# Part of the sparse tokens' first-level choice moved into the query projection, with the end of the picks and a load order changed

## The reference

```python
def peer_ffn(h, w_query, sub_keys, expert_u, expert_v):   # shortened
    q = (xt @ w_query).reshape(T, 8, 2, 128)               # 8 heads, 2 halves: 16 rows a token
    scores = einsum('thpc,hpnc->thpn', q, sub_keys)         # 128 keys for each of the 16 rows
    top_s, top_i = top_k(scores, 16)                        # FIRST level: 16 of 128, 16 times a token
    cand_s = top_s[:, :, 0, :, None] + top_s[:, :, 1, None, :]
    best_s, best_pos = top_k(cand_s..., 16)                 # SECOND level: 16 pairs a head
    idx  = ...                                              # 8 x 16 = 128 experts a token, of 16384
    gate = softmax(best_s)
    y = sum over the 128: gate * gelu(x . expert_u[idx]) * expert_v[idx]
```

## Time and profile before

| | us |
|---|---|
| median of 3 runs (2687.11 to 2694.08) | 2687.2 |
| the profiled execution, its own time | 2686.54 |
| its span, from which all rows are | 2684.8 |
| PE busy | 2316.3 (86%) |
| DVE busy | 1514.0 (56%) |
| ACT busy | 631.7 (24%) |
| POOL busy | 601.3 (22%) |

### The profile page before, as it was taken

The page is one execution under the profiler, slowest core; times in us unless marked ns, Lnnn a source line. Parts: engine busy times, 40 slices in busy tenths (PEclk is TensorE's granted clock), DMA queues, the critical chain, the costliest instruction groups (busy, mean ns, idle before and its releaser), DMA issues. The chain is left out here.

```text
span 2684.8 us, 42381 instructions
## 1 busy us (share of the span) xinstructions
PE 2316.3 (86%) x16668; PEld 1693.7 (63%) x16668; DVE 1514.0 (56%) x2992; ACT 631.7 (24%) x1540; POOL 601.3 (22%) x637
## 2 busy tenths in 40 slices
PE   8989988999998689997998788768998799788873
PEld 8988865555554387886964445428788796455431
DVE  5787643110000155588966666675558896666666
ACT  4543322000000035222311111114622231111111
POOL 0011200111111100001234545530000123545553
PEclk9999989999999989999999999999999899999998
DMA  7420026999999781379999999978137899999996
GB/s 230 144 68 3 3 110 249 401 419 419 418 420 419 316 288 32 118 255 364 361 398 408 407 405 411 389 279 287 32 118 281 341 377 397 407 411 405 410 387 254
DMA packets 223238, 794.92 MB, mean 296 GB/s; under 512 B 37909, under 2 KB 103957, under 8 KB 165312
## 3 DMA queue, kind: packets, MB, share of 16 engines
q1 hardware_dynamic: 148496, 443.86, 43.0%
q0 software_dynamic: 74544, 348.34, 32.9%
HBM read 881.07 MB, written 11.27 MB: 332 GB/s over the span
## 5 line engine op out<-in xcount | busy, mean ns | idle before, releaser
L2472 PE MATMUL psum<-v_raw,act 128*128 128x512 f32 x1024 | 504.9, 624 | 168.7 <-DMA v_raw<-expert_v_dram,all_gates 168.4
L2439 PEld LDWEIGHTS psum<-all_gates 128*128 128x128 f32 x4096 | 491.6, 195 | 103.8 <-issue 58.4
L2439 PE MATMUL psum<-all_gates 128*128 128x128 f32 x4096 | 499.8, 279 | 39.6 <-DMA all_gates<-expert_u_dram 39.1
L2582 POOL DMA_INDIRECT all_gates<-expert_pairs_dram,all_gates x256 | 261.8, 1023 | 1143.0 <-DVE all_gates L2718 533.5
L2472 PEld LDWEIGHTS psum<-v_raw,act 128*128 128x128 f32 x1024 | 181.5, 194 | 407.9 <-DMA v_raw<-expert_v_dram,all_gates 261.5
L2618 DVE CUSTOM_DVE_ANT_0 all_gates<-all_gates,psum 128x1024 f32<-128x1024 f32 x204 | 249.1, 1221 | 307.5 <-DMA all_gates<-expert_pairs_dram,all_gates 307.4
L2629 DVE SCALAR_TENSOR_TENSOR psum<-all_gates,psum 128x1024 f32<-128x1024 f32 x254 | 326.3, 1285 | 8.1 <-ACT all_gates L2543 7.8
L1741 PE MATMUL psum<-piece_raw,tile_cols 128*64 128x256 f32 x2496 | 289.3, 383 | 17.9 <-DMA piece_raw<-w_up_dram 7.8
L1741 PEld LDWEIGHTS psum<-piece_raw,tile_cols 128*64 128x64 f32 x2496 | 177.2, 137 | 130.3 <-issue 36.7
L2590 POOL DMA_INDIRECT v_raw<-expert_v_dram,all_gates x236 | 234.5, 994 | 77.7 <-issue 69.0
L2541 ACT ACTIVATE all_gates<-all_gates 128x1 f32<-128x1 f32 x256 | 51.8, 202 | 770.8 <-DVE all_gates L2618 770.5
(11 more groups left out here) (530 smaller groups left out, 3405.0 us busy)
## 6 DMA issues: line engine op xcount, KB each, us to landing
all_gates<-expert_u_dram SPq DMA_DIRECT2D x256, 512.0 KB, 7.7
piece_raw<-w_gate_dram SPq DMA_DIRECT2D x78, 1024.0 KB, 19.5
piece_raw<-w_up_dram SPq DMA_DIRECT2D x78, 1024.0 KB, 21.6
piece_raw<-w_down_dram SPq DMA_DIRECT2D x78, 1024.0 KB, 22.8
in_raw<-w_in_dram SPq DMA_DIRECT2D x48, 1024.0 KB, 5.2
query_raw<-w_query_dram SPq DMA_DIRECT2D x16, 1024.0 KB, 5.6
v_raw<-expert_v_dram SPq DMA_DIRECT2D x20, 512.0 KB, 8.1
w_o<-w_o_dram SPq DMA_DIRECT2D x16, 512.0 KB, 10.2
```

The lines of the kernel that those rows point to most:

```text
L2439: last = nc.tensor.matmul(PS[:, bank, 0:P], raw_u[:, n % RAW_U, c * P:(c + 1) * P], h_full[:, c, :], start=(c == 0), stop=(c == KD - 1), s ...
L2472: last = nc.tensor.matmul(PS[:, 4 + m, :], slot(n), raw_v[:, n % RAW_V, m * BANK:(m + 1) * BANK], start=(n == 0), stop=(n == N - 1), skip_ ...
L2582: nc.gpsimd.indirect_dma_start(out=ring[:, r, :, :].rearrange("p h d -> p (h d)"), out_offset=None, in_=S["pair_rows"], in_offset=bass.Ind ...
```

## The change

- `query` gets six banks for its units, and the other two for scores. Behind units 1, 3, 4, 5 and 6, PE computes the sparse tile's scores of one head each (heads 0 to 4), ACT copies them out, and DVE makes that head's first-level choice behind its work for the next slab. So 10 of the 16 rows of the sparse tile's first level are done when `small_experts` begins, and `select(0)` handles 6. PE waits for the keys before the first of these. An extra phase with three semaphores is put around `query`.
- `select(1)` takes 15 picks in between instead of 10, two of them in the middle of long groups. The loop has 97 picks left instead of 102, and they end with its step 121 instead of 126.
- `EARLY` is 68 instead of 72, `LISTS_AFTER` 41 instead of 46, and the shares and the exponentials on ACT stand behind earlier dense blocks.
- `want()`, which finds the v rows that are needed, is called one step later in the loop.
- `in2` issues its ten `loads` after all 12 slabs, not between them.

```diff
 def project(..., busy=(0, 0, 0, 0), loads_last=False, heads=None):
-                    if s >= RING:
+                    if s >= RING and not loads_last:
                         for buffer, src in loads[(s - RING) * share:(s - RING + 1) * share]:
                             sp.dma_start(buffer, src).then_inc(loaded, 16)
+                for buffer, src in loads if loads_last else ():
+                    sp.dma_start(buffer, src).then_inc(loaded, 16)
...
+                    if heads and n in heads.behind:        # ACT, last in unit n
+                        heads.scalar(act, heads.behind.index(n))
...
+                    if heads and n in heads.behind:        # DVE, behind low_of_slab
+                        heads.vector(dve, heads.behind.index(n))
...
+                    if heads and n in heads.behind:        # PE, behind unit n
+                        if n == heads.behind[0]:
+                            pe.wait_ge(loaded, 16 * len(loads))
+                        if act_upto[n]:
+                            pe.wait_ge(unit_act, act_upto[n])
+                        pe.wait_ge(unit_dve, n - act_upto[n])
+                        heads.tensor(pe, heads.behind.index(n))
...
+HEADS_BEHIND = (1, 3, 4, 5, 6)
+class FirstChoice:
+    def tensor(self, pe, h):      # two 128x128 products into bank 6 + h % 2
+    def scalar(self, act, h):     # waits for them, copies 256 columns to S["sc"]
+    def vector(self, dve, h):     # waits for the copy
+        for i in two: last = nc.vector.max(val[:, i, 0:8], sc[:, 1, i, :])
+        step(last)
+        for i in two: last = nc.vector.max_index(...)
+        step(last)
+        for i in two: last = nc.vector.match_replace(...)
+        step(last)
+        for i in two: last = nc.vector.max(val[:, i, 8:16], ...)
+        step(last)
+        for i in two: last = nc.vector.max_index(...)
...
-EARLY = 72
+EARLY = 68
...
-    EXP_AFTER = (14, 41)
-    LISTS_AFTER = 46
+    CHOSEN_FIRST = (2 * len(HEADS_BEHIND), 0)
+    BATCHES = tuple(range(c // 4, 4) for c in CHOSEN_FIRST)
+    EXP_AFTER = (8, 38)
+    LISTS_AFTER = 41
-    SHARES_AFTER = (24, 26, 30, 33, 34, 36, 39, 41, 43, 44)
+    SHARES_AFTER = (19, 20, 21, 23, 24, 26, 28, 29, 30, 32, 34, 35, 36, 38, 39)
-    LAST_BLOCKS = 2
+    LAST_BLOCKS = 7
...
-                    waiting = [None, None, *range(BESIDE_CHOICE)] if a == DENSE else []
+                    waiting = list(range(BESIDE_CHOICE)) if a == DENSE else []
+                    open_rows = range(CHOSEN_FIRST[turn], HP)
...
-                    if n == 0:
+                    if n == 1:
                         want()
...
-                        loads=loads, banks=(0, 1), ring=3, act_from=8,
+                        loads=loads, loads_last=True, banks=(0, 1), ring=3, act_from=8,
...
-                    above=3 * 16 * KB)
+                        above=3 * 16 * KB, banks=(0, 1, 2, 3, 4, 5),
+                        heads=FirstChoice(nc, S, head_scored, head_copied, head_chosen))
```

More of the change, by code:

```diff
@@ L196, in project @@
             raw=None, banks=tuple(range(BANKS)), ring=2, act_from=None, beside=None, norm=None,
-            ahead=None, above=0, tops_early=False, extra=None, late_loads=(), also=None, busy=(0, 0, 0, 0)):
+            ahead=None, above=0, tops_early=False, extra=None, late_loads=(), also=None, busy=(0, 0, 0, 0), loads_last=False, heads=None):
     PS, C = S["psum"], S["const"]
@@ L2271, in layer_norm, with __init__, bank, step @@
             nc.vector.tensor_scalar(norm["diag"][:, a, :], norm["ident"], norm["rstd"][:, a:a + 1], None, ALU.mult)
+HEADS_BEHIND = (1, 3, 4, 5, 6)
+class FirstChoice:
+    def __init__(self, nc, S, scored, copied, chosen):
+        self.nc, self.S, self.behind = nc, S, HEADS_BEHIND
+        self.scored, self.copied, self.chosen, self.steps = scored, copied, chosen, 0
+    def bank(self, h):
+        return self.S["psum"][:, 6 + h % 2, 0:2 * P]
+    def tensor(self, pe, h):
+        S = self.S
+        if h >= 2:
+            pe.wait_ge(self.copied, h - 1)
+        for e in range(2):
+            last = self.nc.tensor.matmul(self.bank(h)[:, e * P:(e + 1) * P], S["q_cols"][:, 2 * h + e, P:2 * P],
+                                         S["keys"][:, 2 * h + e, :], start=True, stop=True)
+        last.then_inc(self.scored, 1)
+    def scalar(self, act, h):
+        act.wait_ge(self.scored, h + 1)
+        self.nc.scalar.activation(self.S["sc"][:, 1, 2 * h:2 * h + 2, :], self.bank(h).rearrange("p (i n) -> p i n", n=P),
+                                  ACT.Copy).then_inc(self.copied, 1)
+    def vector(self, dve, h):
+        nc, sc, val, idx = self.nc, self.S["sc"], self.S["val"], self.S["idx"]
+        two = range(2 * h, 2 * h + 2)
+        def step(ins):
+            self.steps += 1
+            ins.then_inc(self.chosen, 1)
+            dve.wait_ge(self.chosen, self.steps)
+        dve.wait_ge(self.copied, h + 1)
+        for i in two:
+            last = nc.vector.max(val[:, i, 0:8], sc[:, 1, i, :])
+        step(last)
+        for i in two:
+            last = nc.vector.max_index(idx[:, i, 0:8], val[:, i, 0:8], sc[:, 1, i, :])
+        step(last)
+        for i in two:
+            last = nc.vector.match_replace(sc[:, 1, i, :], val[:, i, 0:8], sc[:, 1, i, :], NEG)
+        step(last)
+        for i in two:
+            last = nc.vector.max(val[:, i, 8:16], sc[:, 1, i, :])
+        step(last)
+        for i in two:
+            last = nc.vector.max_index(idx[:, i, 8:16], val[:, i, 8:16], sc[:, 1, i, :])
 def one_row(S, name, layer):
     return S["dram"][name][bass.ds(layer, 1), :].rearrange("l n -> (l n)").partition_broadcast(P)
-EARLY = 72
+EARLY = 68
 RAW_U, RAW_V = 4, 7
@@ L2338, in small_experts @@
         keys = S["keys"]
-        sc = spare([P, NT, HP, NKEYS])
-        val = spare([P, HP, TOPK])
-        idx = spare([P, HP, TOPK]).bitcast(U32)
+        sc, val, idx = S["sc"], S["val"], S["idx"]
         idx_h = spare([P, PH * TOPK]).bitcast(BF16).rearrange("p (h e k) -> p h e k", h=2, k=TOPK)
@@ L2417, in scores @@
                 def scores(turn, n):
-                    if turn:
-                        pe.wait_ge(scores_out, n + 1)
+                    if turn and n in BATCHES[0]:
+                        pe.wait_ge(scores_out, BATCHES[0].index(n) + 1)
                     a = ORDER[turn]
-                    for i in range(4 * n, 4 * n + 4):
+                    for i in range(max(4 * n, CHOSEN_FIRST[turn]), 4 * n + 4):
                         last = nc.tensor.matmul(PS[:, n, (i % 4) * P:(i % 4 + 1) * P], S["q_cols"][:, i, a * P:(a + 1) * P],
@@ L2477, in back @@
                         last.then_inc(y_done, 1)
-                for n in range(4):
+                for n in BATCHES[0]:
                     scores(0, n)
@@ L2482, in _ @@
                     turn_x(b)
-                for n in range(4):
+                for n in BATCHES[1]:
                     scores(1, n)
@@ L2654, in select @@
                     beside()
-                    for i in range(HP):
+                    for i in open_rows:
                         last = nc.vector.max(val[:, i, 8:16], sc[:, a, i, :])
+                        if i == middle:
+                            beside()
                     step(last)
                     beside()
-                    for i in range(HP):
+                    for i in open_rows:
                         last = nc.vector.max_index(idx[:, i, 8:16], val[:, i, 8:16], sc[:, a, i, :])
+                        if i == middle:
+                            beside()
+                    beside()
                     v = val.rearrange("p (e h) k -> p e h k", h=2)
@@ L2708, in select @@
                         step(last)
-                    beside()
+                        if width != 4:
+                            beside()
                     for h, to in enumerate((rows[:, 0, :], second)):
@@ L3040, in second_layer @@
             between["shift_row"] = spare([P, D])
-            project(nc, S, "query", S["x"], one("w_query_2", "k n"),
-                    [(c, 512, "columns") for c in range(0, 2048, 512)], evacuate=evacuate_q,
-                    raw=ahead["raw"], loads=[(S["keys"], one("sub_keys_2", "p e n"))], norm=between, ahead=ahead,
-                    above=3 * 16 * KB)
+            S["sc"] = spare([P, NT, 2 * PH, NKEYS])
+            S["val"] = spare([P, 2 * PH, TOPK])
+            S["idx"] = spare([P, 2 * PH, TOPK]).bitcast(U32)
+            with phase(nc, "head_scored head_copied head_chosen") as (_, head_scored, head_copied, head_chosen):
+                project(nc, S, "query", S["x"], one("w_query_2", "k n"),
+                        [(c, 512, "columns") for c in range(0, 2048, 512)], evacuate=evacuate_q,
+                        raw=ahead["raw"], loads=[(S["keys"], one("sub_keys_2", "p e n"))], norm=between, ahead=ahead,
+                        above=3 * 16 * KB, banks=(0, 1, 2, 3, 4, 5),
+                        heads=FirstChoice(nc, S, head_scored, head_copied, head_chosen))
```

24 lines of the change are left out of this document (14 added, 10 removed).

## The result

The changed kernel took 2654.91 us (median of four, 2652.71 to 2660.21) against 2689.51 for the kernel before, measured beside it (2687.11 to 2694.08): a ratio of 0.9887, 95% interval 0.9866 to 0.9909, so 30 us or 1.1% faster (25 to 36 us). Forecast were 2661 us, 26 less, with a range of 2648 to 2680. Run again with the last experiments it took 2656.98, ratio 0.9888 (0.9869 to 0.9907). The profiled execution took 2652.92 us with a span of 2651.1.

What follows compares the result with a forecast made beforehand. DMA was taken to bound the expert stage, PE in2 and query. Terms over two layers: in2 -12.9, query +7.4, sparse -11.0, dense -4.4, end -5.0, sum -25.9 from 2686.5, plus 0.7: 2661 us, range 2648 to 2680.

Steps and rivals of the forecast that it cites:

- in2: Projection in2: loads issued last remove PE's gaps and the clock loss behind them, 12.9 us less over both layers.
- query: Query projection: five heads' scores and choices plus an extra phase lengthen it 3.7 us a layer, 7.4 in all.
- the choices: Expert stage's sparse and dense choices: less DMA loss, 11.0 us less in the sparse and 4.4 in the dense.
- the end: End of the expert loop: picks end earlier, PE finishes 5 us behind DMA instead of 8.4; 2.5 us less a layer.
- the slabs are then never late: In in2: without loads between, a slab needs 2.7 us of DMA against a 5.76 us PE unit; all three gaps go.
- the stall of 1.0 before unit 4: In query: DVE's added choice and row work finish a slab late, so PE stalls 1.0 us.
- (e): Rival in query: the choices delay every slab by 2 us, 20 us over both layers, giving 2681; chance 0.06.
- rival (d): Dense choice: picks wait for their shares, DVE's waits for ACT 3 us or more; slower, 2703; chance 0.07.
- the 2.2 us: Dense choice: more picks in flight cut DMA's loss from 8.9 (6.0) to 6.5 (4.0) us, 2.2 a layer.
- (a): Rival: only in2 gives; the expert stage starts 3.7 us later and earlier picks' gain is eaten; 2674; chance 0.20.
- (b): Rival: the dense choice's DMA loss all but vanishes and the end gives 4 us; 2650; chance 0.12.
- (c): Rival: in2 gives nothing because PE waits for the next slab's rest instead of the copy-out; 2674; chance 0.07.

Runs made afterwards that it cites:

- no heads: Changed kernel without the five heads' choice in query, all 16 rows chosen in the expert stage, fifteen picks at later places: 2660.76 us, ratio 0.9909.
- (undone): Changed kernel with LAST_BLOCKS back at 2, so picks run to the second last block: 2666.72 us, ratio 0.9940.
- (alone): Kernel before with LAST_BLOCKS at 7 in place of 2 and nothing else: 2675.02 us, ratio 0.9970.

## Why the prediction was right, and where it was off

**The sum.** In the stages, by means over profiles: in2 -10.9, query +6.2, the choices -14.1, the end -11.1; -29.9 us in all, and the ratio gives -30. Predicted were -12.9, +7.4, -15.4 and -5.0, -25.9. Three terms were each a little too large, and one less than half its size, so the sum came out nearer than its parts.

**in2 (-12.9, measured -10.9).** The mechanism is shown: the gaps behind ACT's copy went from 4.7 and 5.2 to 0.4 and 2.3 us, and the edit alone gives its part. Off was "the slabs are then never late": `w_o` was one of two loads between the slabs. The constants, 641 KB, and some rows stand between the third slab and the fourth, which is asked for at 1805.02 and landed 13 us later. With them moved too, the stage loses 13.2 us over both layers, near what the term said. The late `w_o` cost nothing, as said: in layer 1 it was issued until 1850.2 and took at most 14.1 us, so it was there at 1864.3 at the latest. The stage's last product was at 1886.7, and the prediction's test was that `w_o` lands before it.

**query (+7.4, measured +6.2).** Units stayed at 5.76 us on PE, with no gap ahead of any; the stall of 1.0 before unit 4 didn't come. A head's choice took 2.9 us from its first maximum at 1113.13, under the 3.2 charged and short enough for DVE's copy-out to be in time. The extra phase cost 0.4 (no heads against before), not 0.8. Nothing was seen of (e): its sign, gaps before each unit, didn't appear.

**Sparse and dense choice (-15.4, measured -14.1).** The size came out, but what held the dense choice was not what the prediction said, so part of the agreement is luck. Predicted was a dense choice bound by DMA, with DVE done at 109 and DMA at 115 us behind the stage's start, and waits of DVE for ACT under 1 us. The lists came at 117.6 and 115.4, but held by DVE: PE had all its 41 blocks done and waited 7.0 and 6.1 us for DVE there. DVE was late by its 77 us of work, as sized (65 + 12), by one wait for the first share of 6.05 us (5.0 in layer 1), and by one of 2.5 (1.2) for a pick's rows. By the prediction's own sign, 3 us or more, that is rival (d)'s mechanism, once a layer and not fifteen times.

The wait goes with the first four pick loads: after them the u blocks took 11.9 us from issue to landing in the median in place of 4.6, so the gelu that the share stands behind was late. In the kernel before they slowed as much, from 4.6 to 10.9 us, behind its own first picks, but there the picks came 12 us later against the blocks, with the first share behind `gelu(24)` and not `gelu(19)`, and the first adds waited 0.1 and 1.2 us. That the u blocks slow agrees with the Trainium skill ("DMA: Bandwidth & Descriptors", Queues, rings and completion order), by which each DMA engine takes turns between the queues that have work. The prediction set that rule against the rate and against the 2.2 us. The rate rose all the same, to 391 and 381 GB/s, over the 365 of its test; whether the five picks gave any time isn't resolved. What the slower blocks touched was the order of the shares, which the prediction had among its rivals and not in its sum.

With the shares spread the stages give 4.5 us a layer more; that edit takes the wait out, has three more blocks done and frees ACT, and no run tells these three apart. Of the 7.0 us a layer that the choices gave, the heads hold 3.6 (predicted 5.5) and the five more picks 1.2, unresolved (predicted 2.2); the 2.2 us that are left are not assigned: no run takes both out at once. All three rest on one profile of a run against the mean of others.

**The end (-5.0, measured -11.1).** This is the term that was mis-sized, 2.5 a layer for 5.6 by the expert stages (5.8 by the loops): "PE so ends 5 us behind DMA instead of 8.4: 3.4 us. DMA's rate there may sink, since fewer loads are in flight: I take 2.5". Its first half, 3.4 us, measured 2.6 (undone) and 4.8 (alone), and 4.0 in the two profiles of layer 1 shown above. Counted to the start of the dense half, as the prediction did, the levels are 11.5 and 7.5 us and not 8.4 and 5: the 8.4 counts from the last pick's landing, as if DMA had been full until then, but its bytes end 3.2 us earlier by the count at 400 GB/s. Before, POOL issued each of the last two picks' loads only after a wait for a free buffer, and so for DVE's add, and the last load then took 8.1 us to its dot (timeline of POOL before):

```profile
2649.91 0.99 POOL L2582 DMA_INDIRECT all_gates<-expert_pairs_dram,all_gates  x1 [2.06 <-DVE psum L2629]
...
2653.64 0.99 POOL L2582 DMA_INDIRECT all_gates<-expert_pairs_dram,all_gates  x1 [1.44 <-DVE psum L2629]
```

Nor is it PE alone that ends the layer after: DVE's 8.35 us and PE's last blocks end together. The second half had the wrong sign. I took 0.9 off for a DMA that sinks; instead its work ended sooner, by 1.1 to 3.3 us in the loops, and the loop's rate, 405.3 for 402.7 GB/s, is of that size. Why the rate is higher no run tells; with 7 last blocks the loop has 0.80 picks a block instead of 0.77, which is little. The loss I feared is there, but at 12 blocks, where PE's pace shows.

**The rivals.** (a) would have needed an expert stage that gives back only the query's 3.7; it is 12.6 us shorter, by the means of the table. (b), 2650, lies as near to the measured time as the forecast, and for half its reason: the end gave more than its 4 us a layer. (c) and (e) are out, and (d)'s wait came once a layer, as described above.

## What to carry to other kernels

Where a resource sets the pace, measure its tail by its bytes and not by its last transfer: here the last landing came 3.2 us behind the time by which a full DMA would have moved the same bytes. Let the last transfers be those whose consumer needs least behind them, and stop before the consumer's own pace is the bound (here 4 to 7 blocks, not 2 and not 12). And when work is moved beside other work under a fixed order, look first at the first hand-over: spreading the shares, with three more blocks ahead of the lists, gave 4.5 us a layer in a stage whose DMA was already 98% busy.

## What the runs showed of the hardware

A block of 512 KB on SP's queue took 4.6 us from issue to landing (median of twelve) before four gathers of picks were issued on POOL's queue, and 11.9 us (median of five, up to 14.3) just after, while DMA's total went from 281 to 425 GB/s. The kernel before has the same: 4.6 us (median of 18) and then 10.9 (median of five). In the rest of the stage, with DMA 98% busy, the blocks took 9.5 us (median of 17), so a full DMA may slow them as much as the taking of turns; no run separates the two. PE waited 4.62 us for such a block, from 1187.5 to 1192.1. In the five us from 1190, which hold the end of the wait and what follows, the granted clock was 0.63, so part of them were at the lower of the two levels, and 32 products took 6.86 us where the 32 before the wait had taken 3.74:

```profile
1185.00:1190.00 5.00, 2.48 (x23) 2.29 (x21) 4.97 (x39) 0.56 (x2) 0.45 (x1) 1.00 0.95 361
1190.00:1195.00 5.00, 2.90 (x13) 2.90 (x14) 4.97 (x29) 0.00 (x0) 0.00 (x0) 0.63 1.02 425
```
